# A two-layer hybrid decoder step: gate units run inside the prompt attention, the long convolution inside the gathered selection

## The reference

```
xn   = rms_norm(x)                       # 520 tokens x 1024
proj = xn @ w_in                         # q, six k/v parts, branch gates, conv a, conv c, 3 x 1024 merge gates
B    = nsa(q, k/v, sigmoid(gates))       # compressed + 16 selected blocks of 64 + window of 512
A    = gated short convolution           # 3 taps
C    = swish(layer_norm(conv31(glu)))    # 256 channels, 31 taps
mix  = (sig(g0)*(B@w_nsa_out) + sig(g1)*(A@w_a_out) + sig(g2)*(C@w_c_out)) @ w_o
```

## Time and profile before

| | us |
|---|---|
| median of 3 runs | 3454.62 (3438.43 to 3459.28) |
| the profiled execution | 3444.01, its span 3442.2 |
| prompt attention, first layer | 239.1 to 419.2 |
| ring | 419.2 to 657.4 |
| window, input formed again | 657.4 to 683.1 |
| gathered selection | 683.1 to 812.6 |
| gate stage | 817.6 to 973.4 |
| out stage | 973.4 to 1023.2 |

### The profile page before, as it was taken

How to read it: one execution, slowest core, us unless ns; L and a number is a source line. 1 busy time by engine, 2 the same in 40 slices (tenths; PEclk the granted TensorE clock), 3 DMA queues, 4 the chain that set the end, 5 groups by cost and what they waited for, 6 DMA issues and landing times. The chain is left out here.

```text
span 3442.2 us, 52566 instructions
## 1 busy us (share of the span) xinstructions
PE 2967.0 (86%) x20176; PEld 2686.4 (78%) x20176; DVE 1628.8 (47%) x3316; ACT 973.5 (28%) x2045; POOL 166.4 (5%) x118
## 2 busy tenths in 40 slices
PE   5979799767997788999989797997699976899997
PEld 3966578647997687999988565775489976799997
DVE  4345567535664314554243555764283543345523
ACT  1123355201233113222222333551023321322221
POOL 1000000000003002000020000000000020110001
PEclk8967799767998758999989668996699986689998
DMA  5320065342232302333332103553232331123331
GB/s 155 100 80 13 19 186 178 112 125 62 80 99 74 135 8 67 93 93 92 93 82 71 59 13 99 178 166 106 66 99 80 105 122 44 50 62 92 93 90 58
DMA packets 443905, 309.50 MB, mean 90 GB/s; under 512 B 48726, under 2 KB 429980, under 8 KB 443140
## 3 DMA queue, kind: packets, MB, share of 16 engines
q1 hardware_dynamic: 427028, 292.62, 28.3%
q10 hardware_dynamic: 16640, 13.64, 1.3%
HBM read 295.48 MB, written 19.55 MB: 92 GB/s over the span
## 5 line engine op out<-in xcount | busy, mean ns | idle before, releaser
L310 PE MATMUL pg<-act_hi,w_lo 128*128 128x260 f32 x3072 | 644.0, 292 | 92.2 <-DVE act_lo L401 46.6
L310 PE MATMUL pg<-act_lo,w_hi 128*128 128x260 f32 x3072 | 633.3, 289 | 0.0
L310 PE MATMUL pg<-act_hi,w_hi 128*128 128x260 f32 x3072 | 633.0, 288 | 0.0
L282 DVE TENSOR_TENSOR w_lo<-w_raw,w_hi 128x1024 fp32r<-128x1024 f32 x296 | 368.7, 1246 | 527.6 <-ACT w_hi L275 526.7
L310 PEld LDWEIGHTS pg<-act_hi,w_lo 128*128 128x128 f32 x3072 | 487.9, 194 | 106.4 <-DVE w_lo L282 49.6
L310 PEld LDWEIGHTS pg<-act_lo,w_hi 128*128 128x128 f32 x3072 | 488.8, 195 | 0.0
L310 PEld LDWEIGHTS pg<-act_hi,w_hi 128*128 128x128 f32 x3072 | 488.7, 194 | 0.0
L275 ACT CAST w_hi<-w_raw 128x1024 fp32r<-128x1024 f32 x296 | 309.1, 1045 | 470.9 <-PE pg L310 349.3
L1290 DVE COPY pair<-pg 64x256 f32<-64x256 f32 x512 | 218.4, 427 | 113.7 <-PE pg L1391 58.9
L1391 PE MATMUL pg<-pair,w 128*128 128x256 f32 x1024 | 266.3, 383 | 0.0
L1290 ACT COPY pair<-pg 64x256 f32<-64x256 f32 x512 | 186.4, 364 | 177.6 <-PE pg L1373 103.5
(11 more groups left out here) (438 smaller groups left out, 4237.8 us busy)
## 6 DMA issues: line engine op xcount, KB each, us to landing
ring<-in_cache_kv SPq DMA_DIRECT2D x512, 128.0 KB, 2.2
w_raw<-in_w_ffn_in SPq DMA_DIRECT2D x88, 512.0 KB, 3.7
w_raw<-in_w_in SPq DMA_DIRECT2D x80, 512.0 KB, 3.6
cmem<-in_cache_mem SPq DMA_DIRECT2D x16, 1024.0 KB, 13.4
w_raw<-in_w_ffn_out SPq DMA_DIRECT2D x32, 512.0 KB, 3.5
sel<-in_cache_kv SPq DMA_DIRECT2D x240, 64.0 KB, 2.1
sel<-in_cache_kv ACTq DMA_DIRECT2D x208, 64.0 KB, 2.2
win<-in_cache_win SPq DMA_DIRECT2D x16, 512.0 KB, 5.3
```

What stands on the lines that cost most here:

```text
L282: e.tensor_tensor(w_lo[:, v % 2, :], w_raw[:, v % RING, :], w_hi[:, v % 2, :].bitcast(F32), ALU.subtract).then_inc(w_ready, 1)
L310: mm = e.matmul(pg[:, ts, h, 0:wd], w[:, v % 2, wk], x[:, k0 + k, at:at + wd], start=first and k == 0 and n == 0, stop=last and k == kn - ...
```

## The change

Per layer:

- **Compression stage**: PE spreads the row factors of the norm, DVE forms `act_n`, ACT `act_hi`, DVE `act_lo`; this leaves the window part of the gathered selection.
- **Prompt attention** is written out. The score has one bank (`pg[:, 0]`); the other (`pg[:, 1]`) takes gate units in 96 *quanta* of 12 matmuls, three per step. ACT applies the tanh of a half into one of four slots in `z` and casts the next weights; DVE forms their low part between `read(n+1)` and `normalise(n+1)`; SP writes the slot to DRAM (`gate_dram`) and loads the next raw weights. The copies of queries into `q_i` are dropped.
- **Gathered selection**: a transfer takes the rows of one head group (64 rows of two runs of 64 floats, 32 KB), 15 blocks per sample on each queue instead of 15 and 13; eight places for eight samples, so no wait for `q_pv`. PE turns one 128-row tile per half instead of two, DVE copies it in one piece; PE works `ktile(m)` ahead of `kscore(m-1)`, values come one sample later. DVE carries 20 convolution taps ahead of `o_cw`, four behind each half `m` from 0 to 10; mean, variance and scale of the LayerNorm stand at m = 12, 13, 14; ACT's square and tanh behind its gathers.
- **Gate stage** is dropped; the out stage reads three gate results per unit from DRAM, between the loads of weights.

```diff
@@ prompt attention, SP
+ load_units(e, vg + 1, vg + 6)
+ for n in range(NSTEP):
+     for j in finished(n):
+         u, part = divmod(j, 4)
+         if part == 3:
+             e.wait_ge(gate_ev, 2 * u + 2)
+             e.dma_start(gate_dram.ap()[u], gate_slot(u)).then_inc(g_out[u % GSLOT], 16)
+             if u + 6 <= NG:
+                 load_units(e, vg + u + 6, vg + u + 7)
...
@@ prompt attention, PE
- score(0, 0)
- score(0, 1)
- run(e, trip)          # per step: turn(n), score(n + 2), values(n)
+ def gate(j):
+     u, part = divmod(j, 4)
+     h, late = divmod(part, 2)
+     v = vg + u
+     if part == 0:
+         e.wait_ge(w_ready, v + 1)
+     if late == 0 and u:
+         e.wait_ge(gate_ev, 2 * u + h - 1)
+     for k in range(4 * late, 4 * late + 4):
+         wk = slice(k * P, (k + 1) * P)
+         for m, (w, x) in enumerate(((w_lo, act_hi), (w_hi, act_lo), (w_hi, act_hi))):
+             mm = e.matmul(pg[:, 1, h, 0:HALF], w[:, v % 2, wk], x[:, k, h * HALF:(h + 1) * HALF], ...)
+ score(0)
+ for j in range(EACH):
+     gate(j)
+ for n in range(NSTEP):
+     turn(n)
+     if n + 1 < NSTEP:
+         score(n + 1)
+     for at_, j in enumerate(quanta(n)):
+         if at_ == 1:
+             values(n)
+         gate(j)
...
@@ prompt attention, DVE
+ for n in range(NSTEP):
+     copy(n)
+     if n + 1 < NSTEP:
+         read(n + 1)
+     for j in finished(n):
+         if j % 4 == 3:
+             split_lo(e, vg + j // 4 + 2) if j // 4 + 2 <= NG else None
+     if n + 1 < NSTEP:
+         normalise(n + 1)
+     keep(n)
...
@@ prompt attention, ACT
+ for n in range(NSTEP):
+     copy(n)
+     if n + 1 < NSTEP:
+         exps(n + 1)
+     gates(n)            # tanh of finished halves, then split_hi of the next unit
...
@@ gather
- row, count = 8 * g + b, 15 - 2 * g
+ row, count = 8 * g + b, 15
- elif b >= 4:
-     e.wait_ge(q_pv, (b - 4) // 2 + 1)
- e.dma_start(sel[half * 64:half * 64 + 64, place[b % 4], tile, g, :], rows_kv[bass.ds(start[k], 64), :])
+ e.dma_start(sel[half * 64:half * 64 + 64, place[b], tile, :, g * HD:(g + 1) * HD], rows_kv[g, bass.ds(start[k], 64)])
...
- exps_in = {3: (0, 0), 5: (1, 4), 7: (2, 6)}
+ exps_in = {3: (0, 6), 5: (1, 6), 7: (2, 6)}
...
@@ gathered selection, PE
+ for m in range(2 * NB + 1):
+     if m < 2 * NB:
+         ktile(m)
+     if m:
+         kscore(m - 1)
+     if m >= 5 and m % 4 == 1:
+         pturn(m // 4 - 1)
+     if m >= 6 and m % 4 == 2:
+         values(m // 4 - 1)
+     if m in also:
+         also[m]()       # conv_mean, conv_variance, conv_spread
+ pturn(NQ - 1)
+ values(NQ - 1)
...
@@ out stage, SP and DVE
- load_units(e, v0 + U_MG + 1, v0 + U_WO)
+ for m in range(KC):
+     for i in range(3):
+         e.dma_start(G[:, m + KC * i, :], gate_dram.ap()[m + KC * i]).then_inc(g_in[m], 16)
+     load_units(e, v0 + U_OUT + 1 + m, v0 + U_OUT + 2 + m)
...
+ e.wait_ge(g_in[m], 48)
  merge(e, m)
```

More of the change, by code:

```diff
@@ L950, in _ @@
                     def _(e):
+                        for tt in range(5):
+                            w, at_ = (P, tt * P) if tt < 4 else (NB, SEQ)
+                            cut = ident[:] if tt < 4 else ident[:, P - NB:P]
+                            mm = e.matmul(N0.bc[:, at_:at_ + w], N0.r[:, tt:tt + 1].broadcast_to([P, P]), cut, start=True, stop=True)
+                        mm.then_inc(rn_bc, 1)
                         e.wait_ge(pr_used, 8)
@@ L1063, in turn @@
+                        def turn(n):
+                            i, g, t, s, r, w, nc_ = step(n)
+                            e.wait_ge(probs, n + 1)
+                            if n:
+                                e.wait_ge(ptr_used, 2 * n)
+                                e.wait_ge(ptc_used, n)
                             for b in range(2):
                                 for kt in range(t + 1):
-                                    mm = e.transpose(pn[:, b, kt * P:(kt + 1) * P], s_lg[:, k % 2, b, kt * P:(kt + 1) * P], ident[:])
@@ L1087, in trip @@
-                        def trip(i, last=False):
-                            for k in range(STEPS):
-                                turn(i, k)
-                                if not (last and k >= STEPS - 2):
-                                    score(*after(i, k, 2))
-                                values(i, k)
+                            e.wait_ge(ptc_used, n + 1)
+                            e.matmul(out, cv[0:nc_, r], pTc[0:nc_, s, :], start=False, stop=True).then_inc(pv, 1)
+                        def gate(j):
[9 more added lines that the diff above has]
+                                for m, (w, x) in enumerate(((w_lo, act_hi), (w_hi, act_lo), (w_hi, act_hi))):
+                                    mm = e.matmul(pg[:, 1, h, 0:HALF], w[:, v % 2, wk], x[:, k, h * HALF:(h + 1) * HALF],
+                                                  start=k == 0 and m == 0, stop=k == KC - 1 and m == 2)
+                            if part == 1:
+                                mm.then_inc(gate_half, 1)
+                            if part == 3:
+                                mm.then_inc(unit_done, 1)
@@ L1155, in trip @@
-                        def trip(i, last=False):
-                            for k in range(STEPS):
-                                dve_chain.restart(e)
-                                normalise(i, k)
-                                if not (last and k == STEPS - 1):
-                                    read(*after(i, k, 1))
-                                copy(i, k)
-                                if not (isinstance(i, int) and i == k == 0):
-                                    keep(*after(i, k, -1))
@@ new lines, in _ @@
+                        split_lo(e, vg + 1)
+                        read(0)
+                        normalise(0)
+                        for n in range(NSTEP):
[8 more added lines that the diff above has]
+                            keep(n)
@@ L1200, in trip @@
-                        def trip(i, last=False):
-                            for k in range(STEPS):
-                                copy(i, k)
-                                if k == STEPS - 2 and not last:
-                                    queries(i + 1)
-                                if not (last and k == STEPS - 1):
-                                    exps(*after(i, k, 1))
-                                copy_compressed(i, k)
-                        queries(0)
-                        exps(0, 0)
```

562 lines of the change are left out of this document (259 added, 303 removed).

## The result

The changed kernel takes 3371.5 us (median of 4 runs, 3368.6 to 3381.1) against 3452.3 for the kernel before (4 runs, 3438.4 to 3459.3): a ratio of 0.978, with a 95% interval of 0.976 to 0.980. The forecast was 3378.

The account below looks back on a forecast made before the run. TensorE's pauses and lowered clock in the attention, and pure TensorE work in the gate stage, were taken as bounds. Per layer 125 - 156 - 10 + 4 + 4 = -33, twice -66 from 3444.0: 3378 us, range 3345 to 3420.

Parts of the forecast that it names:

- The gates move under the softmax: Gate matmuls go into the prompt attention: attention +125 us per layer (306 against 181), gate stage gone, -156.
- The chain's sum: Prompt attention: steps of 8.5, 9.2, 8.1 and 11.6 us, mostly set by softmax and weight splits; 37.4 a group, 299 for eight.
- The entry: Start of the prompt attention: first step waits for the second unit's weights; with the last values 7 us (4 to 10).
- PE's own work: Prompt attention: TensorE's work at full clock, 8.2 us per step on the mean, 262 us for 32 steps.
- faster rival: Prompt attention: the chain is short and PE alone bounds, 262 + 7 = 269 us; kernel 3304 us; chance 0.09.
- The rival on the clock: Prompt attention: clock stays at 0.77, 347 us, +41 per layer; kernel 3460 us; chance 0.14.
- the slow rival: Prompt attention: gate quanta hide nothing, all comes on top of the steps, 374 us, +68 per layer; kernel 3514; chance 0.10.
- The gather: Gathered selection ends near 803 instead of 812.6 on the timeline: -10 us per layer (between -25 and +10).
- the 90 us of issuing per queue: Gather: 15 issues per sample and queue, eight samples need 90 us per queue, without waits for free places.
- the three exponentials: Gather: exponentials between ACT's transfers, each waiting for a pair's scores; 5 us allowed for each.
- The taps: Gather: the convolution's 62 taps, 64 us of DVE, hidden under the gates before, stay hidden.
- Compression: Compression stage: renormalised input made before the attention, mostly beside the stage's own waits; +4 us (0 to 16).

Follow-up runs that it names:

- the second try: Changed kernel with a pair's last score, softmax and values ahead of the next keys, exponentials one sample earlier, squares on DVE, five taps behind three of four halves: 3407.5 us.

## Why the prediction held, step by step

- **The gates move under the softmax** (+125 against -156): measured +120.1 and +116.0 against -154. The mechanism, PE's pauses filled and its clock raised, is shown from three sides: full quanta 0.97 and 303 us, half 0.81 and 0.73 with 312 and 332, one matmul 0.56 and 334; and inside one layer the same half quanta take 33.5 us a group at full clock and 41.0 at 0.71.
- **The chain's sum was right in total and off in its parts.** 37.4 us a group came out as 35.9, 12 less in eight groups. The entry, put at 7 with the last values, was 12.5 for the first transposes alone, and the first group took 4.3 more than the others; these are some 9 more than the sum has. That the two errors nearly cancel is luck. The chain does bound the steps to t=1 and t=3, as said (the run with half quanta), but it was overstated by 1 us in each, and PE's own work was understated, 32.8 against the 34.4 of the run with the low part last. So the chain reaches beyond PE's work by only 1.5 of 35.9 us; with the low part moved PE bounds alone. The forecast's faster rival had that at 269 us, and the runs show it at 281.8, with the early load.
- **The rival on the clock** priced the gate work at the clock of before. In these runs the clock moved with the work that was put in (0.77 before, 0.97 now), as the prediction's own argument against this rival had it. The same holds for the slow rival: its "hide nothing" had to assume work that leaves the clock where it is.
- **The gather**: -10 came out as -6.4 and -6.0. The term that failed is the 90 us of issuing per queue, at the pace of before. 120 issues took 107.4 us on SP, 0.895 each, where the earlier trace rows gave 0.75:

```profile
786.28 107.40 SPq L1373 DMA_DIRECT2D sel<-in_cache_kv  x120
```

  That is 17 us more, and twice the runs per transfer make 13 of them (94.1 us on SP in the run with long runs). Most of it came back: both queues started 2 us after the choice, where the sum had 6 for ACT, and the three exponentials held ACT by a few us in all instead of 15. So the last landing was at 113 us after the choice and not 112, and behind it came 35 us, forecast 34. Here too the parts were off and the total near, by luck.
- **The taps** are hidden, as said, shown by the run without them. That ACT's gathers can wait behind a DVE queue full of taps (in the second try PE idled 3.9 us for a key copy behind five) was not seen.
- **Compression** +3.8 against +4. It can be read off ACT's first copy and SP's first load of the next stage, before:

```profile
225.99 2.54 ACT L946 COPY pairs<-z 64x256 f32<-64x256 f32 x4 [8.68 <-PEq L793]
...
239.12 0.85 SPq L1025 DMA_DIRECT2D toep_h<-toep_scratch  x2
```

  and after, with ACT's casts between:

```profile
229.58 2.55 ACT L941 COPY pairs<-z 64x256 f32<-64x256 f32 x4 [8.69 <-PEq L773]
...
239.78 2.20 ACT L927 CAST act_hi<-act_n 128x520 fp32r<-128x520 f32 x4
...
242.05 2.19 ACT L927 CAST act_hi<-act_n 128x520 fp32r<-128x520 f32 x4
...
246.52 0.83 SPq L1045 DMA_DIRECT2D toep_h<-toep_scratch  x2
```

## What to carry to other kernels

Look at the granted clock of a stage before counting the cost of added matmuls: where PE pauses and the clock is low, independent products put into the pauses can cost far less than their time at full clock (13.7 us for 40 in the kernel before), and the last of them less than nothing (the second half of each quantum). A stage full of PE work that follows is the place to take them from. When work of a second stream is put into an in-order queue, place it behind what the first stream's next step needs (the low part behind normalise: 14 to 15 us per layer), and start its first loads a stage early. Where an engine both computes and issues transfers, every wait in front of its arithmetic delays all transfers behind it: of two reorderings of the gather that looked shorter on paper, one gained nothing and one lost 15 us a layer, and in both ACT's last transfers left later.

## What was not expected of the hardware

- Leaving work out made a stage longer: eleven of twelve gate matmuls less, 303.3 to 333.7 us, at a clock of 0.56 instead of 0.97. Within one kernel the two layers of the run with half quanta ran the same stage in 311.7 us at 0.81 and 331.6 at 0.73.
- The gather's issuing instruction takes longer with more runs at the same bytes: 599 ns for 128 runs of 256 bytes, 469 for 64 runs of 512 bytes, and also 469 for 64 runs of 1 KB in the kernel before:

```profile
L1340 SPq DMA_DIRECT2D sel<-in_cache_kv x240: 468/469/1457, 659.0 to 2452.0; - x120
```

  The landing time hardly follows (2.2, 2.0 and 2.1 us). It is no price per run for every transfer: on the same queue a weight load of 512 KB, 1024 runs of 512 bytes, is issued in 368 ns (the kernel before). What else of a transfer's form sets the time is open.
